# Sharing gate and up pieces between two chunks of an expert, and another layout of its down pieces, in a decoder trunk

## The reference

```
gates = one_hot(top_idx) * softmax(top_val)          # (256, 8), two entries a row
for each expert e:
    hg = x @ w_gate[e]        # (256,1024) @ (1024,3584)
    hu = x @ w_up[e]          # (256,1024) @ (1024,3584)
    hh = silu(hg) * hu * gates[:, e]
    y += hh @ w_down[e]       # (256,3584) @ (3584,1024)
```

## Time and profile before

| what | value |
|---|---|
| time, median of 3 runs | 1386.95 us (1386.16 to 1394.77) |
| the profiled execution's own time | 1392.87 us |
| its span, first to last instruction | 1391.1 us |
| granted TensorE clock, mean | 0.952 |
| PE busy | 1251.6 us, 90% of the span |
| HBM read | 411.38 MB, 296 GB/s over the span |
| chain that ended last, by engine | PE 81%, DMA 8%, issue 6%, DVE 4%, ACT 2% |

### The profile page before, as it was taken

How to read it: one execution, slowest core, us unless ns; L and a number is a source line. 1 busy time by engine, 2 the same in 40 slices (tenths; PEclk the granted TensorE clock), 3 DMA queues, 4 the chain that set the end, 5 groups by cost and what they waited for, 6 DMA issues and landing times.

```text
span 1391.1 us, 20342 instructions
## 1 busy us (share of the span) xinstructions
PE 1251.6 (90%) x8591; PEld 639.3 (46%) x8592; DVE 334.6 (24%) x741; ACT 267.5 (19%) x490; POOL 28.2 (2%) x43
## 2 busy tenths in 40 slices
PE   6999999999998898999788987899969888799997
PEld 4765777787664533444332332334433233233443
DVE  2354666676343300110010010020001001002002
ACT  2232333332261010111110110111111011011111
POOL 2100000000100100000000000000000000000000
PEclk9979999999999799999989999999998999999999
DMA  9511744347333299999979999999997999999991
GB/s 341 174 53 32 272 170 164 104 171 261 131 122 127 103 376 400 389 393 396 390 275 394 397 390 393 400 389 393 397 388 296 394 397 390 395 399 390 393 398 63
DMA packets 173127, 413.83 MB, mean 297 GB/s; under 512 B 4166, under 2 KB 9404, under 8 KB 172780
## 3 DMA queue, kind: packets, MB, share of 16 engines
q1 hardware_dynamic: 171660, 409.58, 78.8%
q0 software_dynamic: 1088, 1.81, 0.4%
q10 hardware_dynamic: 288, 1.05, 0.2%
HBM read 411.38 MB, written 1.05 MB: 296 GB/s over the span
## 4 chain that ended last, share of the span: by engine, by line
PE 81%; DMA 8%; issue 6%; DVE 4%; ACT 2%; SPq 0%; POOL 0%; POOLq 0%; ACTq 0%; DVEq 0%
PE ps L1302 16%; PE ps L1280 16%; PE ps L1284 8%; DMA ring<-in_moe_w_up 7%; PE ps L1345 6%; PE ps L1041 4%; PE ps L1037 4%; PE ps L1038 4%; PE ps L1317 3%; PE ps L1273 3%; PE ps L1022 2%; PE ps L1213 2%; PE ps L1161 2%; PE ps L1330 1%; PE ps L908 1%
## 5 line engine op out<-in xcount | busy, mean ns | idle before, releaser
L1302 PE MATMUL ps<-ring,arena 128*64 128x512 f32 x560 | 265.6, 632 | 54.8 <-DMA ring<-in_moe_w_up 27.8
L1303 PE MATMUL ps<-ring,arena 128*64 128x512 f32 x560 | 265.9, 632 | 0.0
L1280 PE MATMUL ps<-ring,arena 128*32 128x512 f32 x1512 | 261.9, 593 | 1.4 <-issue 1.4
L1281 PE MATMUL ps<-ring,arena 128*32 128x512 f32 x504 | 258.0, 594 | 0.0
L1302 PEld LDWEIGHTS ps<-ring,arena 128*64 128x64 f32 x560 | 79.1, 145 | 229.9 <-issue 193.8
L1284 PE MATMUL ps<-ring,arena 128*32 128x256 f32 x2016 | 155.4, 379 | 0.0
L1284 PEld LDWEIGHTS ps<-ring,arena 128*32 128x32 f32 x2016 | 66.5, 110 | 149.8 <-issue 149.8
L1346 PE MATMUL ps<-ring,arena 128*64 128x512 f32 x280 | 126.6, 598 | 0.0
L1345 PE MATMUL ps<-ring,arena 128*64 128x512 f32 x280 | 126.6, 598 | 0.0
L1784 DVE TENSOR_TENSOR arena<-arena 64x512 f32<-64x512 f32 x35 | 24.7, 707 | 382.7 <-ACT arena L830 382.7
L1556 DVE TENSOR_TENSOR w_lo<-ring,w_hi 128x2048 fp32r<-128x2048 f32 x33 | 75.6, 2292 | 60.2 <-ACT w_hi L727 58.7
(11 more groups left out here) (276 smaller groups left out, 1381.0 us busy)
## 6 DMA issues: line engine op xcount, KB each, us to landing
ring<-in_moe_w_up SPq DMA_DIRECT2D x56, 2048.0 KB, 21.3
ring<-in_moe_w_down SPq DMA_DIRECT2D x56, 2048.0 KB, 19.5
ring<-in_moe_w_gate SPq DMA_DIRECT2D x55, 2048.0 KB, 19.5
ring<-in_ffn_w_gate SPq DMA_DIRECT2D x5, 2048.0 KB, 7.9
ring<-in_ffn_w_up SPq DMA_DIRECT2D x5, 2048.0 KB, 7.9
ring<-in_ffn_w_down SPq DMA_DIRECT2D x5, 2048.0 KB, 7.8
ring<-in_mla_w_o SPq DMA_DIRECT2D x2, 2048.0 KB, 23.8
ring<-in_swa_w_q SPq DMA_DIRECT2D x2, 2048.0 KB, 8.4
```

What stands on the lines that cost most here:

```text
L1280: pe.matmul(ps[32 * j:32 * j + 32, bank, :], thirds[j], left, start=first, stop=last)
L1281: pe.matmul(ps[SLOTS:P, bank, :], thirds[2], right, start=first, stop=last)
L1302: pe.matmul(ps[0:NARROW, 2 * a, :], lhs, wg[:, k, :], start=(k == 0), stop=(k == KD - 1))
L1303: mm = pe.matmul(ps[64:64 + NARROW, 2 * a + 1, :], lhs, wu[:, k, :], start=(k == 0), stop=(k == KD - 1))
```

## The change

The seven chunks are taken as three pairs and one chunk alone. A gate or up piece of a pair holds four rows a partition by 1024 columns: part 0 is rows 0 to 3 of each partition's eight, part 1 rows 4 to 7, and both serve the two chunks of the pair. The seventh chunk keeps its pieces. PE waits for part 0 before step 0 of the even chunk and for part 1 before step 4, and for nothing in the odd chunk. Part 0 is used up at step 3 of the odd chunk (the new semaphore `half_mm`), part 1 at its end. The order of the pieces is now pair 0 (g u of part 0, g u of part 1), pair 1, d0 d1, pair 2, d2 d3, g6 u6, d4 d5 d6. A down piece has the same 512 rows, but a partition holds four neighbours, 16 KB that lie together in HBM; so `hidden_T` takes every fourth hidden column. The piece loaded ahead is now the up piece of pair 1, part 1, and GpSimd waits for `half_mm`.

```diff
@@ the order of pieces, where they lie, and when they are used up
-        pieces = [("g", 0), ("u", 0), ("g", 1), ("u", 1)]
-        for c in range(2, ECH):
-            pieces += [("g", c), ("u", c), ("d", c - 2)]
-        pieces += [("d", ECH - 2), ("d", ECH - 1)]
+        PAIRS = ECH // 2
+        def pair_pieces(n):
+            return [(kind, n, part) for part in range(2) for kind in "gu"]
+        pieces = pair_pieces(0) + pair_pieces(1) + [("d", 0, 0), ("d", 1, 0)]
+        pieces += pair_pieces(2) + [("d", 2, 0), ("d", 3, 0)]
+        pieces += [(kind, PAIRS, 0) for kind in "gu"] + [("d", c, 0) for c in range(4, ECH)]
...
+        def chunk_row(kind, c, k):
+            if c // 2 == PAIRS:
+                return piece(kind, PAIRS, 0)[:, k, :]
+            return piece(kind, c // 2, k // 4)[:, k % 4, (c % 2) * FC:(c % 2 + 1) * FC]
+        def piece_source(kind, n, part, expert):
+            if kind == "d":
+                return ed[:, expert, n]
+            w = eg if kind == "g" else eu
+            if n == PAIRS:
+                return w[:, expert, :, 2 * n * FC:(2 * n + 1) * FC]
+            return w[:, expert, 4 * part:4 * part + 4, 2 * n * FC:2 * (n + 1) * FC]
+        def emptied(m):
+            kind, n, part = pieces[m]
+            if kind == "d":
+                return s.down_mm, ECH, n + 2
+            if n == PAIRS:
+                return s.gu_mm, ECH, ECH + 1
+            if part == 0:
+                return s.half_mm, PAIRS, n + 2
+            return s.gu_mm, ECH, 2 * n + 3
...
-        ed = e_down[0].rearrange("e (k p) n -> p e k n", p=P)
+        ed = e_down[0].rearrange("e (c p j) n -> p e c j n", p=P, j=4)
@@ SyncE, load_item
-                        k0, c0 = pieces[m - RING]
-                        sp.wait_ge(s.down_mm if k0 == "d" else s.gu_mm, i * ECH + (c0 + 2))
...
+                        sem, each, at_item = emptied(m - RING)
+                        sp.wait_ge(sem, i * each + at_item)
+                    sp.dma_start(piece(kind, n, part), piece_source(kind, n, part, expert)).then_inc(slot_landed[expert_slots[m % RING]], 16)
@@ GpSimd
-            pool.wait_ge(s.gu_mm, 2)
+            pool.wait_ge(*(emptied(0)[n] for n in (0, 2)))
@@ PE, products
-                piece_here(pe, i, "g", c)
-                piece_here(pe, i, "u", c)
...
                 for k in range(KD):
+                    if c == 2 * PAIRS and k == 0 or c % 2 == 0 and c < 2 * PAIRS and k % 4 == 0:
+                        piece_here(pe, i, "g", c // 2, k // 4)
+                        piece_here(pe, i, "u", c // 2, k // 4)
+                    wg, wu = chunk_row("g", c, k), chunk_row("u", c, k)
...
+                    if c % 2 == 1 and k == 3:
+                        mm.then_inc(s.half_mm, 1)
                 mm.then_inc(s.gu_mm, 1)
@@ PE, hidden_T
-                    mm = pe.transpose(ps[:, 4, j * SLOTS:(j + 1) * SLOTS], hh[0:SLOTS, c % 2, j * P:(j + 1) * P], ident[0:SLOTS, 0:SLOTS])
+                    mm = pe.transpose(ps[:, 4, j * SLOTS:(j + 1) * SLOTS], hh[0:SLOTS, c % 2, :].rearrange("m (p j) -> m j p", j=4)[:, j, :], ident[0:SLOTS, 0:SLOTS])
```

More of the change, by code:

```diff
@@ L232, in __init__ @@
         self.down_mm = sem("down_mm")
+        self.half_mm = sem("half_mm")
         self.y_ready_a = sem("y_ready_a")
@@ L501, in build, with piece_here, piece @@
         dense_fills = [slot_of.count(sl) for sl in range(RING)]
-        def piece_here(eng, i, kind, c):
-            m = ppos[(kind, c)]
+        def piece_here(eng, i, kind, n, part):
+            m = ppos[(kind, n, part)]
             sl = expert_slots[m % RING]
             eng.wait_ge(slot_landed[sl], i * (16 * NP // RING) + 16 * (dense_fills[sl] + m // RING + 1))
-        def piece(kind, c):
-            sl = expert_slots[ppos[(kind, c)] % RING]
-            return ring[:, sl, :].rearrange("p (k n) -> p k n", k=4 if kind == "d" else KD)
+        def piece(kind, n, part):
+            sl = expert_slots[ppos[(kind, n, part)] % RING]
+            deep = 4 if kind == "d" or n < PAIRS else KD
+            return ring[:, sl, :].rearrange("p (k n) -> p k n", k=deep)
+        def chunk_row(kind, c, k):
[18 more added lines that the diff above has]
+            return s.gu_mm, ECH, 2 * n + 3
         eg = e_gate[0].rearrange("e (k p) f -> p e k f", p=P)
         eu = e_up[0].rearrange("e (k p) f -> p e k f", p=P)
-        ed = e_down[0].rearrange("e (k p) n -> p e k n", p=P)
+        ed = e_down[0].rearrange("e (c p j) n -> p e c j n", p=P, j=4)
         def x_gained(t, b):
@@ L571, in load_item @@
             def load_item(i, expert, first):
-                for m, (kind, c) in enumerate(pieces):
+                for m, (kind, n, part) in enumerate(pieces):
                     if first and m == RING - 2:
                         sp.wait_ge(s.spT_mm, AH)
[L575 to L578, removed]
+                        a_kind, a_n, a_part = pieces[AHEAD]
+                        assert a_kind != "d" and a_n < PAIRS
+                        sp.dma_start(ahead.rearrange("p (k n) -> p k n", k=4),
+                                     piece_source(a_kind, a_n, a_part, expert)).then_inc(s.ahead_loaded, 16)
                     if first and m == AHEAD:
@@ L585, in load_item @@
                         else:
-                            k0, c0 = pieces[m - RING + NP]
-                            sp.wait_ge(s.down_mm if k0 == "d" else s.gu_mm, i * ECH + (c0 + 2 - ECH))
-                    else:
-                        k0, c0 = pieces[m - RING]
-                        sp.wait_ge(s.down_mm if k0 == "d" else s.gu_mm, i * ECH + (c0 + 2))
[L591 to L595, removed]
+                            sem, each, at_item = emptied(m - RING + NP)
+                            sp.wait_ge(sem, i * each + (at_item - each))
+                    else:
+                        sem, each, at_item = emptied(m - RING)
+                        sp.wait_ge(sem, i * each + at_item)
+                    sp.dma_start(piece(kind, n, part), piece_source(kind, n, part, expert)).then_inc(slot_landed[expert_slots[m % RING]], 16)
             load_item(0, 0, True)
@@ L1297, in products @@
                     pe.wait_ge(s.hh_ready, i * (2 * ECH) + (2 * max(c - 1, 0) + 1))
-                wg, wu = piece("g", c), piece("u", c)
                 for k in range(KD):
+                    if c == 2 * PAIRS and k == 0 or c % 2 == 0 and c < 2 * PAIRS and k % 4 == 0:
+                        piece_here(pe, i, "g", c // 2, k // 4)
+                        piece_here(pe, i, "u", c // 2, k // 4)
+                    wg, wu = chunk_row("g", c, k), chunk_row("u", c, k)
                     if narrow:
                         lhs = xgT[:, k, 0:NARROW]
[L1302 to L1305, removed]
+                        pe.matmul(ps[0:NARROW, 2 * a, :], lhs, wg, start=(k == 0), stop=(k == KD - 1))
+                        mm = pe.matmul(ps[64:64 + NARROW, 2 * a + 1, :], lhs, wu, start=(k == 0), stop=(k == KD - 1))
+                    else:
+                        mm = wide_step(2 * a, xgT[:, k, :], wg, wu, k == 0, k == KD - 1)
+                    if c % 2 == 1 and k == 3:
+                        mm.then_inc(s.half_mm, 1)
                 mm.then_inc(s.gu_mm, 1)
@@ L1329, in hidden_T @@
                 for j in range(4):
-                    mm = pe.transpose(ps[:, 4, j * SLOTS:(j + 1) * SLOTS], hh[0:SLOTS, c % 2, j * P:(j + 1) * P], ident[0:SLOTS, 0:SLOTS])
+                    mm = pe.transpose(ps[:, 4, j * SLOTS:(j + 1) * SLOTS], hh[0:SLOTS, c % 2, :].rearrange("m (p j) -> m j p", j=4)[:, j, :], ident[0:SLOTS, 0:SLOTS])
                 mm.then_inc(s.tr_mm, 1)
             def down(i, c, narrow):
-                piece_here(pe, i, "d", c)
+                piece_here(pe, i, "d", c, 0)
                 pe.wait_ge(s.hhT_ready, i * ECH + (c + 2))
@@ L1339, in down @@
                     pe.wait_ge(s.h_added, i * 4 + 4)
-                w = piece("d", c)
+                w = piece("d", c, 0)
                 for j in range(4):
@@ L1350, in down @@
                 mm.then_inc(s.down_mm, 1)
-            for q in (s.gu_mm, s.tr_mm, s.down_mm, s.gath_mm, s.sgt_mm, s.scat_mm):
+            for q in (s.gu_mm, s.half_mm, s.tr_mm, s.down_mm, s.gath_mm, s.sgt_mm, s.scat_mm):
                 pe.sem_inc(q, 1)
```

## The result

The changed kernel takes 1430.97 us (median of 4 runs, 1428.81 to 1433.61) against 1390.23 for the kernel before in runs beside it. The ratio is 1.0267, 95% interval 1.0242 to 1.0292: **slower by 2.7%**, about 37 us by this ratio; the two medians are 40.7 us apart, and the four runs before lie in two groups (1386 to 1387, 1394 to 1395). The forecast was 1397, slower by 10, with a range up to 1414; the time lies outside.

What follows compares the result with a forecast made beforehand. Narrow items were taken as bound by the stream, wide ones by PE. Terms -15.0 + 7.0 + 14.4 + 3.4 = +9.8 us on the profiled 1392.87 gave 1402.7; with the median 5.9 lower, 1397, range 1372 to 1414.

Steps and rivals of the forecast that it cites:

- The stream's rates: Weight loads: 409 GB/s with 4 KB rows; 16 KB rows taken at the 8 KB pace, 426 GB/s.
- (b): Wide items: pieces needed at chunk 0's middle come late, PE waits; 4.8 us each, between 0 and 6.4, +14.4 in all.
- the second wait: Wide items, chunk 4's second half: after the stream pauses 3 to 6 us, PE waits 1 to 3 us.
- the slower PE: Wide items: PE runs slower for a while after a pause, 0 to 1.7 us more, and the second wait shrinks.
- (a): After a wide item, the stream's restart moves from chunk 0's end to chunk 1's middle: +3.5 us, twice, +7.0.
- the gain: From a restart to the second narrow item's last gate and up piece, longer rows save 7.5 us, twice: -15.0.
- the third rival: Ring runs dry in narrow items: gaps of 0.6 to 2.3 us, up to 20 us on top, 1416; chance 0.12.
- (c): Item 0: the ninth and 12th pieces are issued later, so the last up piece ends later: +3.4 us.
- (d): One more wait per half chunk and one more semaphore on PE cost nothing.
- (e): Transposes in wide items read weights at a step of four words: 0 to 13.4 us, taken as 0.
- a rival of doubled blocks: Wide items' transpose loads cost double, block at 0.96 us: +10.1 us, 1407; chance 0.22.
- The first rival: Engines' backlog hides (b), (c)'s pause and most of (a), leaving -17 us: 1370; chance 0.13.

Runs made afterwards that it cites:

- interleaved wide items alone: The changed kernel, with PE taking first halves of both chunks of a pair, then second halves, in wide items only: 1396.26 us, ratio 1.0011.
- the interleaved kernel: The changed kernel, with PE taking first halves of both chunks of a pair, then second halves, in all items; loads untouched: 1384.90 us, ratio 0.9942.
- its better version: The interleaved kernel, with VectorE writing hidden rows permuted so transposes load adjacent columns again, 16 KB down rows kept: 1378.70 us, ratio 0.9887.
- early need alone: The interleaved kernel, early release kept, with PE waiting for part 1 before the odd chunk's first half: 1388.44 us, ratio 0.9953.

## Why the prediction was wrong, by its steps

- **The stream's rates: right.** 4 KB rows gave 408 GB/s, 16 KB rows 431, where 409 and 426 were taken.
- **(b), the wide items: the step that failed, a term mis-sized.** It was put at 4.8 us each, at most 6.4; the wide items grew by 13.3, 10.3 and 10.2. The mechanism, the places and the first wait were right (3.4 predicted; 3.96, 3.94 and 3.62 seen). What failed are the 1.4 us that were to hold the second wait and the slower PE together.
  - *The second wait* was 3.38, 2.90 and 2.87. It had been counted at 1 to 3, and the count itself gives 2.9 when the 2.6 us of a landing are on: the piece lands at 72.9 + 1 + 3 x 5.13 + 2.6 = 91.9, and PE wants it at 72.9 + 5.2 + 0.5 + 5.2 + 5.2 = 89.0. The stream did stop (DMA share 0.00 from 622 to 624), and no backlog hid it.
  - *The slower PE* had been put at 0 to 1.7, and as something that shrinks the second wait. It can't shrink it: the first slow stretch is over by 589, and the slot comes free at 623.75 by PE's own work, so what delays the need delays the freeing as much. It came behind all six waits (from the end of each wait):
```profile
584.08:589.00 4.92, 4.92 (x40) 2.15 (x44) 0.00 (x0) 0.00 (x0) 0.00 (x0) 0.65 1.03 410
643.34:649.50 6.16, 6.16 (x40) 2.15 (x44) 0.00 (x0) 0.00 (x0) 0.00 (x0) 0.53 1.01 426
942.09:948.00 5.91, 5.91 (x52) 2.62 (x56) 0.00 (x0) 0.00 (x0) 0.00 (x0) 0.71 1.03 410
1000.87:1006.00 5.13, 5.13 (x44) 1.87 (x48) 0.00 (x0) 0.00 (x0) 0.00 (x0) 0.69 1.00 425
1297.17:1303.00 5.83, 5.83 (x52) 2.61 (x56) 0.00 (x0) 0.00 (x0) 0.00 (x0) 0.71 1.02 407
1355.92:1361.50 5.58, 5.58 (x52) 2.18 (x56) 0.00 (x0) 0.00 (x0) 0.00 (x0) 0.72 1.00 423
```
  As an estimate, length times the clock that is missing from 1 gives 11.2 us over the six. With 20.7 of waits, where the kernel before had 1.4, and 21 x 0.18 = 3.8 for the transpose blocks, that adds up to 34.3, against 33.8 measured.
- **(a) and the gain: -15.0 + 7.0 forecast, 0 seen.** The restart moved as said: the issue after the first wide item is at 735.27, 10.5 us behind the start of the narrow item, for 7.2 before. The other 4 us of each pair of narrow items went the way of the third rival: late releases open gaps of up to 1 or 2 us (DMA share 0.54 from 788 to 790, 0.46 from 866 to 868; no such slice in these items before). It was real, at 4 us a pair of items and not up to 20 in all. The run with interleaved wide items alone shows the same from the other side: 11 us over the fully interleaved one. In that one, which releases early, the two pairs take 203.7 and 202.2 us: 10.5 of the 15.0 that were forecast for the longer rows.
- **(c): +3.4 forecast, +1.3 seen.** (d): nothing, and nothing seen.
- **(e), the strided loads: taken at 0, with a rival of doubled blocks at +10.1.** The block was misread: the 224 records over 56 blocks are four loads and four matmuls, not eight of each. Seen: loads of 218 ns for 140, a block of 0.66 us for 0.48, +3.8 by the blocks. With the down layout alone the wide items grew by only 0.7, 0.1 and 0.1 us, which fits the blocks only in part: the kernel before lost 1.4 us in its wide products to short waits, this one none. The rule of the Trainium skill (SBUF — State Buffer, the note on cachelines) has the right sign: this trace agrees that a 16-byte step costs, by 78 ns on a load of 128 columns and not by a factor of two on the block. In the whole kernel it weighs nothing that the down layout alone could show (1.0006).
- **The first rival, only the stream counts:** refuted for this kernel, but there was something to be had: with the holding gone the interleaved kernel gains 0.6% and its better version 1.1%.

## What to carry to other kernels

When a load is shared by two steps of work, count for a ring both the moment when it is first needed and the moment when it is given back, in the order in which the consumer really works, other steps between included. One of the two shifts may be covered; here the two together were not, and they cost several times their sum (4.0% of the ratio for 0.1 and 1.0, each of these uncertain by 0.3 to 0.4). Count also what a wait costs behind itself: here 11 us of slower PE came on top of 21 us of waits. Before giving up larger transfers, try another order of the work, so that a shared piece is used by both its users back to back.

## What the runs showed of the hardware that I had not expected

- Behind each of the changed kernel's six waits in wide products (2.87 to 3.96 us) PE fell to a granted clock of about 0.50 for some us, at once or about 2 us later; the mean over the 5 to 6 us behind a wait was 0.53 to 0.72. In the kernel with early need alone, three waits of 2.76 to 2.80 us left the clock at 1.00 and the wide matmuls at 593 ns.
- A multiply on VectorE that writes 64x512 floats with neighbours 128 words apart took 1058 ns (mean) where the contiguous one took 684.
- HBM reads kept rising with the row: 387 GB/s at 2 KB, 408 at 4 KB, 431 at 16 KB (the last over 7 us only; other windows of 7 to 10 us there give 421 to 435).
